# Second block of a two-block model on one core: the order of VectorE's work in the projections and the scan, and the PSUM banks of the down projection

## The reference, cut to what matters

```python
for l in range(2):
    xn = rms_norm_2(h, norm1_g[l])
    z, xbc, dt_raw, q, k, v, gate_logits = split(xn @ w_in[l])
    y_ssd = ssd_mixer(z, xbc, dt_raw, ...)    # causal convolution, chunked scan, * silu(z), group norm
    q, k = rotary(rms_norm_2(q, q_norm_g)), rotary(rms_norm_2(k, k_norm_g))
    y_attn = sliding_window_attention(q, k, v, sinks)
    merged = g_ssd * (y_ssd @ w_ssd_down[l]) + g_attn * (y_attn @ w_attn_down[l])
    h = h + merged @ w_o[l]
    h = h + square(relu(rms_norm_2(h, norm2_g[l]) @ w_mlp_up[l])) @ w_mlp_down[l]
```

## Time and profile before

| what | us |
|---|---|
| median of three runs (lowest, highest) | 3122.3 (3122.02, 3126.4) |
| the profiled execution, its own time | 3129.11 |
| its span, first to last instruction | 3127.8 |
| PE busy | 3021.3 (97%) |
| PEld, DVE, ACT, POOL busy | 2632.8, 1809.1, 1478.5, 1131.2 |
| mean granted clock of PE, share of full | 0.992 |
| HBM read | 455.66 MB, 146 GB/s over the span |

### The profile page before, as it was taken

How to read it: one execution, slowest core, us unless ns; L and a number is a source line. 1 busy time by engine, 2 the same in 40 slices (tenths; PEclk the granted TensorE clock), 3 DMA queues, 4 the chain that set the end, 5 groups by cost and what they waited for, 6 DMA issues and landing times.

```text
span 3127.8 us, 49696 instructions
## 1 busy us (share of the span) xinstructions
PE 3021.3 (97%) x20396; PEld 2632.8 (84%) x20396; DVE 1809.1 (58%) x3211; ACT 1478.5 (47%) x2501; POOL 1131.2 (36%) x440
## 2 busy tenths in 40 slices
PE   7999999998999999999999999999999999999999
PEld 5878887776788886799999877778999978779999
DVE  2377775566676646577465455654465366654554
ACT  3443333444443324665465446554365456554553
POOL 0322232110323231245455423434555424334554
PEclk9999999999999999999999999999999999999999
DMA  9346652211357632178355433334555433335554
GB/s 309 110 163 199 201 189 95 68 54 32 108 198 253 245 131 73 43 263 270 122 164 186 138 108 95 108 95 140 170 162 170 147 95 109 108 109 162 162 187 137
DMA packets 410705, 459.92 MB, mean 147 GB/s; under 512 B 8688, under 2 KB 389616, under 8 KB 410480
## 3 DMA queue, kind: packets, MB, share of 16 engines
q1 hardware_dynamic: 407392, 453.32, 44.7%
q10 hardware_dynamic: 3088, 3.42, 0.3%
HBM read 455.66 MB, written 1.05 MB: 146 GB/s over the span
## 4 chain that ended last, share of the span: by engine, by line
PE 85%; DVE 9%; ACT 4%; issue 1%; DMA 1%; ACTq 0%; POOL 0%; DVEq 0%
PE bank L434 23%; PE bank L436 23%; PE bank L435 23%; ACT wh L381 2%; DVE wl L397 1%; PE banks L434 1%; PE banks L436 1%; PE banks L435 1%; PE bank L638 1%; DVE bc L2586 1%; PE banks L2549 1%; PE banks L478 1%; PE bank L1424 1%; DMA X<-in_ctxT 1%; PE banks L1770 1%
## 5 line engine op out<-in xcount | busy, mean ns | idle before, releaser
L409 POOL TENSOR_TENSOR wl<-raw,wh 128x768 fp32r<-128x768 f32 (+2 forms) x336 | 1013.4, 3016 | 1826.7 <-ACT wh L381 1826.7
L381 ACT ACTIVATE wh<-raw 128x2048 fp32r<-128x2048 f32 (+1 forms) x336 | 636.0, 1893 | 474.9 <-PE bank L436 407.9
L397 DVE TENSOR_TENSOR wl<-raw,wh 128x1280 fp32r<-128x1280 f32 (+2 forms) x336 | 492.7, 1466 | 506.2 <-ACT wh L381 505.9
L434 PE MATMUL bank<-nh,wh 128*128 128x272 f32 (+1 forms) x1712 | 506.8, 296 | 3.4 <-DVE nl L2134 2.8
L436 PE MATMUL bank<-nh,wl 128*128 128x272 f32 (+1 forms) x1712 | 494.2, 289 | 0.0
L435 PE MATMUL bank<-nl,wh 128*128 128x272 f32 (+1 forms) x1712 | 492.7, 288 | 0.0
L434 PE MATMUL bank<-xh,wh 128*128 128x512 f32 (+2 forms) x1282 | 442.6, 345 | 4.2 <-DVE xl L772 3.7
L436 PE MATMUL bank<-xh,wl 128*128 128x512 f32 (+2 forms) x1282 | 434.9, 339 | 0.0
L435 PE MATMUL bank<-xl,wh 128*128 128x512 f32 (+2 forms) x1282 | 434.8, 339 | 0.0
L434 PE MATMUL bank<-hh,wh 128*128 128x512 f32 (+1 forms) x1024 | 344.1, 336 | 0.0
L435 PE MATMUL bank<-hl,wh 128*128 128x512 f32 (+1 forms) x1024 | 344.1, 336 | 0.0
(11 more groups left out here) (462 smaller groups left out, 5589.9 us busy)
## 6 DMA issues: line engine op xcount, KB each, us to landing
raw<-in_mlp_w SPq DMA_DIRECT2D x128, 1024.0 KB, 5.4
raw<-in_w_in SPq DMA_DIRECT2D x60, 1024.0 KB, 5.3
raw<-in_mod_wT SPq DMA_DIRECT2D x44, 1024.0 KB, 5.1
extra<-in_mod_wT SPq DMA_DIRECT2D x32, 1024.0 KB, 5.3
raw<-in_w_mlp_up SPq DMA_DIRECT2D x32, 1024.0 KB, 5.4
raw<-in_w_mlp_down SPq DMA_DIRECT2D x32, 1024.0 KB, 4.9
raw<-in_w_in SPq DMA_DIRECT2D x34, 512.0 KB, 4.7
raw<-in_w_ssd_down SPq DMA_DIRECT2D x16, 1024.0 KB, 4.9
```

The source lines that it names most:

```text
L381: nc.scalar.activation(self.wtile(self.wh, c1), self.rawtile(c1), AF.Copy).then_inc(*up("act_wh", ("wh", c1)))
L397: nc.vector.tensor_tensor(l, r, h.bitcast(F32), ALU.subtract).then_inc(*up("dve_wl", ("wl_dve", c1)))
L409: nc.gpsimd.tensor_tensor(l, r, h.bitcast(F32), ALU.subtract).then_inc(*up("pool_wl", ("wl_pool", c1)))
L434: nc.tensor.matmul(o, ah, bh, start=first, stop=False)
```

## The change

Three edits, all in the second block. In `dve_proj` the norms of an iteration stand first, the window's scaling behind them, and the split of the even iterations up to g = 4 behind the gate product; from g = 6 on the order is as before. In `dve_ssd` all four weighings of a group stand at step i = 1. In `pe_merge` the down projection takes banks 4 and 5, then 6 and 7, in turn. No instruction is added or taken away.

```diff
--- before.py
+++ after.py
@@ -2297,10 +2297,6 @@
         nc.vector.memset(self.sm[:, 0:96], 0.0).then_inc(*up("dve_const", ("sm0", l)))
         DVE.wait_ge(*at("table2"))
         for g in range(16):
-            if g - 1 in self.STEP:
-                self.dve_window_scale(l, self.STEP[g - 1])
-            if g % 2 == 0:
-                self.dve_split(self.ix["z", l, g // 2])
             for i in (2 * g, 2 * g + 1):
                 if i < 10:
                     k = self.HEADS[i]
@@ -2309,9 +2305,15 @@
                     DVE.wait_ge(*at("raw2", l, k))
                     nc.vector.scalar_tensor_tensor(out=dst, in0=dst, scalar=self.col(gain, l), in1=self.place["hn", l, k][:, 0:LT], op0=ALU.mult, op1=ALU.mult
                                                    ).then_inc(*up("dve_hn", ("roped", "h", l, k), ("out", "hn", l, k)))
+            if g - 1 in self.STEP:
+                self.dve_window_scale(l, self.STEP[g - 1])
+            if g > 4 and g % 2 == 0:
+                self.dve_split(self.ix["z", l, g // 2])
             DVE.wait_ge(*at("zs", l, g))
             nc.vector.scalar_tensor_tensor(out=self.y[:, g, REAL[l]], in0=self.u[4 + g % 2][:, REAL[l]], scalar=1.0, in1=self.place["z", l, g][:, REAL[l]],
                                            op0=ALU.add, op1=ALU.mult).then_inc(*up("dve_zm", ("zm", l, g), ("out", "z", l, g)))
+            if g <= 4 and g % 2 == 0:
+                self.dve_split(self.ix["z", l, g // 2])
             for i in (2 * g - 2, 2 * g - 1):
                 if 0 <= i < 10:
                     k = self.HEADS[i]
@@ -2692,9 +2694,9 @@
                 if g == 8 and i % 2 == 0:
                     self.dve_split(self.ix["g1" if i == 0 else "ad", l, 0])
                 if g:
-                    if 1 <= i <= 2:
-                        self.dve_weigh(l, 4 * (g - 1) + 2 * i - 2)
-                        self.dve_weigh(l, 4 * (g - 1) + 2 * i - 1)
+                    if i == 1:
+                        for u in range(4):
+                            self.dve_weigh(l, 4 * (g - 1) + u)
                     if i >= 2:
                         self.dve_skip(l, 2 * (g - 1) + i - 2)
                 if g == 8 and i >= 2:
@@ -2736,7 +2738,7 @@
             for m in range(2):
                 self.pe_group(c, m, slot, X, T, ("g0", l, 2 * j + m), m == 1)
         for j in range(4):
-            os = [self.pe_bank((4, 5), "sd", l, 2 * j + m)[:, T] for m in range(2)]
+            os = [self.pe_bank(((4, 5), (6, 7))[j % 2], "sd", l, 2 * j + m)[:, T] for m in range(2)]
             for r in range(2):
                 c = self.ix["sd", l, j, r]
                 h, lo = self.pe_take(c)
```

## The result

The changed kernel takes 3098.53 us (median of four runs, 3093.19 to 3105.42), the kernel before in the same session 3124.35 us (four runs, 3122.02 to 3127.15). The ratio is 0.9919, with a 95% interval from 0.9902 to 0.9936. That is 25.8 us less, of 26.0 forecast, and 2.5 us above the 3096.0 of the forecast, inside its range. The profiled execution took 3098.32 us.

What follows compares the result with a forecast made beforehand. TensorE, busy 97% of the span, was taken as the bound, so only its idle time or slowed clock could be won. 9.0 + 10.5 + 6.5 = 26.0 us off the 3122.3 median gave 3096, range 3086 to 3108.

Steps and rivals of the forecast that it cites:

- Part 1: Projections: norms ahead of the split shorten PE's rope waits and avoid clock falls; 9.0 us, bounds 3.0 and 18.9.
- the 2.3 + 2.5 of the forecast: Projections, layer 0: 0.7 us of wait plus 1.6 of clock at g = 2, and 2.5 us at g = 4.
- I take the 1.6 us as won: Projections, g = 2: about 0.9 us idle remains, yet the clock does not fall; 1.6 us per layer, bounds 0 and 1.6.
- the prediction's signs of being wrong: L397 in the scan over 1.49 us with L409 first, a scan wait on another line, or clock 0.5 at new places.
- a measure of idle time that the clock bears: Clock stayed at 1.00 with 2.0 us of 8 idle, fell after 1.4 of 4; 0.9 was judged nearest the first.
- Rival 1: Projections: the clock falls stay at g = 2, leaving 22.8 us won, 3099.5 us; chance 0.13.
- Part 2: Scan: earlier weighings free the state matmuls' bank 0.4 us before PE asks; all 14 waits go, 10.5 us.
- Rivals 3: Scan: a next wait takes half or all of the 10.5 us, 3101.5 to 3107 us; chance 0.10.
- 4: Scan: late weighings let GpSimd go ahead of VectorE's split; 9.1 us lost instead of 10.5 won, 3116; chance 0.04.
- 5: Scan: GpSimd first, with a clock fall behind each wait; 31.5 us lost, 3138 us; chance 0.02.
- Part 3: Down projection: alternating bank pairs give the gate product a whole pair of PE work; six waits go, 6.5 us.
- Rival 6: Down projection: the clock swings as banks go round, costing 51 us, 3147 us; chance 0.01.

Runs made afterwards that it cites:

- the first execution: The profiled execution of the changed kernel, nothing further edited; 3098.32 us.
- e5: The changed kernel profiled again, nothing edited (the second execution); 3093.61 us, one execution.
- e1: The kernel before with only the new order in the projections (`dve_proj`); 3117.48 us, 0.9975 of before.
- e8: The kernel before with unread matmuls filling its long rope waits, four at g = 2 and seven at g = 4; 3119.84 us, 0.9984 of before.
- e2: The kernel before with only the weighings of the scan moved (`dve_ssd`); 3115.66 us, 0.9964 of before.
- e4: The changed kernel with the split of g = 0, 2 and 4 ahead of the gate product again, behind the norms; 3100.85 us, 0.9907 of before.
- e7: e4 with the split of g = 4 moved behind the window's maxima of g = 5; 3090.08 us, 0.9884 of before.
- e6: The changed kernel with unread matmuls ahead of the ropes of g = 1 and 2 and in the y norm; 3094.8 us, 0.9897 of before.
- e9: e7 with one or two unread matmuls at four places where PE waits; 3090.69 us, 0.9896 of before.

## Why the prediction was right, and where its sum was off

**Part 1, projections: forecast 9.0 us; 6.7 in the first execution, 8.2 in the second.** The waits are as foretold: 0.81 at g = 1 (forecast 0.7), 0.93 at g = 2 where the clock is not low already (0.9), none at g = 4, and the split there takes 2.60 us behind GpSimd's 1.84 (2.5). With no fall, layer 0 gives 4.79 (e5) and 4.84 us (e1), the 2.3 + 2.5 of the forecast; layer 1 gives 4.05 of 4.2 in the first execution, whose one fall there, behind g = 5, was mostly taken up by the wait behind it. The step that failed is the clock at g = 2: "I take the 1.6 us as won". The price was right (e8: 1.5 us), and behind g = 2 of layer 0 the clock did stay at 1.00 (3.39 us), but the fall came at other places; of the prediction's signs of being wrong, this is the one that came. The prediction drew from two windows a measure of idle time that the clock bears; e1 has a fall in the very place of the first of them, and e5 has other falls than the same kernel's first execution. In that first execution a fall stood behind the 0.81 us wait that the change itself makes at g = 1, and a second one stood behind a 1.29 us wait that the kernel before had passed without. Rival 1 had the right size for such an execution, but the wrong reason: the falls don't stay at g = 2.

**Part 2, scan: forecast 10.5; measured 11.5, in every kernel that has this part** (in e2 and e4 less a fall of 1.5 at the end of layer 0's scan). All 14 waits went; the split stands 0.28 us behind the weighings (forecast 0.3) and the bank is free 0.4 us before PE asks (0.4). Rivals 3, 4 and 5 did not come: L397 stays at 1.49 us and 0.05 us ahead of L409. The term was 1.0 us too small, and the overlap that PE loses by a wait, which its row leaves out, would account for it.

**Part 3, down projection: forecast 6.5; measured 7.9** in each of six kernels, for the same reason, 0.23 us for each of six waits. Rival 6 did not come: 48.10 of 48.10 us busy at 1.00. Here the rule that the prediction weighed (the Trainium skill, TensorE: Matmul & The Clock Gate, section on psum-queue depth-cycling) did not show: going round four banks left PE no gap here.

**What no part named:** the y norm gave 2.9 us in the first execution and 0.2 in the second. Its waits are the same 0.54 and 0.98 us in every kernel that does not fill them, and e2, which touches nothing there, gave 1.8: with the same waits, what differs in the rows is how long the clock stays at the lower level.

So the sum of 26.0 met the 25.8 us between the medians partly by luck: 2.4 us too little in parts 2 and 3, against 0.8 to 2.3 us too much in part 1, and a y norm that gives 0 to 3 us by chance. The rest of the scatter, the first block's 0 to 7.6 us, is larger than any of these.

**Where the change left time:** at g = 1 and at g = 4. At g = 1 the wait that the change itself makes is gone when the split of g = 0 stands ahead of the gate product (e4 and e7), 0.67 us in layer 0. At g = 4 GpSimd's 1.84 us and VectorE's split exclude each other in either order, as e4 shows, and a split that is out of the ropes' way wins 1.2 us more in each layer. e7, which has both, is 8.5 us faster than the change by the medians (3090.08 and 3098.53), of which the projections explain 2.8 to 4.3 (11.0 against 8.2 and 6.7 in the two executions of the change). The rest lies in code that e7 does not touch; the scatter of the falls and of the first block is large enough for it, but no run shows that it is that.

## What to carry to other kernels

- Read a wait's row as a lower bound: each short wait of PE in the scan and the down projection cost 0.07 to 0.23 us more than its row (the lost overlap would account for it).
- A fall of the clock in one profile is one draw. Price it from rows (1.5 us here), but take it as won only where the wait itself goes, and profile a second execution before a difference of a few us is put down to a place.
- When two engines exclude one another at one instruction, reordering them only picks the one that is held, and what stands next may be held in its place; move one of the two to where its engine waits anyway.

## What was not expected of the hardware

- Matmuls that nobody reads, in waits of 0.5 to 4 us, took away the falls behind them in e6 and e8, and in e9 all but one. They pay only if they end before the wait does: 1.56 us of them in an 0.81 us wait won nothing.
- The clock fell at about 2115.9 in e9 after more than 14.30 us in which PE was never idle, the last 2.6 of them mostly matmuls of 8 rows; no run here shows why.
